# A hybrid recurrence and pooling block on eight cores: the pool group map, its channel scale and the pool part of the branch matrix multiplied into one matrix on the chip

## The reference, cut to what matters

```
proj = rmsnorm(h) @ w_in                      # q | f | i | out-gate | pool | gate_a | gate_b
ya = (rmsnorm_per_head(recurrence(q, f, i)) * sigmoid(og)) @ w_br_hgrn
# pool branch: 4 groups of 128 channels, windows 2, 4, 8, 16
pooled[g] = trailing_mean(xp[g], w_g) - xp[g]
y[g] = pooled[g] @ w_grp[g]                   # 128 x 128 for each group
yb = (y * scale) @ w_br_pool                  # 512 x 1024
h = h + (sigmoid(gate_a) * ya + sigmoid(gate_b) * yb) @ w_out
h = h + (silu(u @ w_gate) * (u @ w_up)) @ w_down      # u = rmsnorm(h), 2816 wide
out = rmsnorm(h)
```

## Time and profile before

| what | value |
|---|---|
| median of 3 runs | 2169.29 us (2168.22 to 2170.08) |
| the profiled execution's own time | 2170.29 us |
| its span, from the first to the last instruction, slowest core (core 5) | 2168.7 us |
| spans of the eight cores | 2158.5 to 2168.7 us |
| PE (matmul) busy | 2088.9 us, 96% of the span |
| DVE, ACT, POOL busy | 1001.8, 1007.0, 574.0 us |
| moved by DMA | 405.24 MB |

### The profile page before, as it was taken

How to read it: one execution, slowest core, us unless ns; L and a number is a source line. 1 busy time by engine, 2 the same in 40 slices (tenths; PEclk the granted TensorE clock), 3 DMA queues, 4 the chain that set the end, 5 groups by cost and what they waited for, 6 DMA issues and landing times.

```text
span 2168.7 us, 38075 instructions; the slowest of 8 cores (2158.5 to 2168.7 us)
## 1 busy us (share of the span) xinstructions
PE 2088.9 (96%) x11476; PEld 1106.8 (51%) x11476; DVE 1001.8 (46%) x1756; ACT 1007.0 (46%) x1492; POOL 574.0 (26%) x671
## 2 busy tenths in 40 slices
PE   6777998999999999999999999999999999999997
PEld 3432554555555555555555555555555555554447
DVE  4644453447534742474246523662357235732223
ACT  4832763258415742464247623662358324731111
POOL 3121120001105251423243143314332414223300
PEclk9988999999999999999999999999999999999999
DMA  9999999887565666557555755575557555565577
GB/s 202 211 198 249 217 223 238 228 213 221 147 183 154 186 190 177 158 156 225 170 151 170 223 162 159 168 222 162 166 164 199 180 173 158 165 175 174 169 197 191
DMA packets 232789, 405.24 MB, mean 187 GB/s; under 512 B 24208, under 2 KB 66704, under 8 KB 232592
## 3 DMA queue, kind: packets, MB, share of 16 engines
q1 hardware_dynamic: 210080, 364.62, 57.6%
q0 software_dynamic: 20880, 36.32, 11.7%
q10 hardware_dynamic: 1632, 1.88, 0.4%
HBM read 385.94 MB, written 53.08 MB: 202 GB/s over the span
## 4 chain that ended last, share of the span: by engine, by line
PE 84%; DMA 12%; SPq 1%; issue 1%; DVE 1%; ACT 1%; POOL 0%; DVEq 0%; POOLq 0%; ACTq 0%
PE psa L496 75%; DMA wsc<-wr 6%; DMA wr<-wpk 5%; PE psa L661 5%; DMA wr<-wsc 1%; PE psa L782 1%; SPq L364 1%; PE psa L796 1%; PE psa L815 1%; PE psa L816 1%; PE psa L831 0%; DMA fa<-xT 0%; PE psa L620 0%; PE psa L601 0%; DVE ba L630 0%
## 5 line engine op out<-in xcount | busy, mean ns | idle before, releaser
L496 PE MATMUL psa<-ba,wr 128*128 128x456 bf16 (+2 forms) x8960 | 1776.7, 354 | 19.8 <-DVE ba L546 6.6
L496 PEld LDWEIGHTS psa<-ba,wr 128*128 128x128 bf16 x8960 | 868.1, 98 | 830.2 <-issue 40.6
L906 DVE TENSOR_TENSOR ba<-psa,fa 128x456 bf16<-128x456 f32 (+1 forms) x198 | 124.5, 631 | 250.8 <-PE psa L496 213.0
L905 ACT ACTIVATE fa<-psa 128x456 f32<-128x456 f32 (+1 forms) x198 | 107.1, 551 | 217.1 <-PE psa L496 185.1
L589 POOL TENSOR_TENSOR fa<-fa 128x456 f32<-128x456 f32 (+1 forms) x160 | 158.0, 996 | 161.8 <-DMA fa<-xT 76.9
L773 POOL TENSOR_TENSOR ba<-fa 128x456 bf16<-128x456 f32 (+1 forms) x48 | 61.1, 1272 | 480.7 <-ACT fa L756 257.9
L363 POOL DMA_DIRECT2D wr<-wpk x145 | 76.8, 535 | 373.8 <-DMA wsc<-wr 180.6
L661 PE MATMUL psa<-wr,ba 128*114 128x512 bf16 (+1 forms) x576 | 136.6, 384 | 3.0 <-DMA wr<-wpk 3.0
L765 DVE TENSOR_TENSOR_SCAN fa<-ba,fa 128x456 f32<-128x456 bf16 (+1 forms) x72 | 83.4, 1159 | 120.1 <-ACT fa L763 120.0
L866 POOL TENSOR_TENSOR fa<-fa 128x456 bf16<-128x456 f32 (+1 forms) x48 | 55.3, 1152 | 289.2 <-DVE fa L863 289.2
L863 DVE SCALAR_TENSOR_TENSOR fa<-fa,psa 128x456 f32<-128x456 f32 (+1 forms) x72 | 45.3, 629 | 165.9 <-PE psa L496 165.9
(11 more groups left out here) (84 smaller groups left out, 1767.2 us busy)
## 6 DMA issues: line engine op xcount, KB each, us to landing
wr<-wsc SPq DMA_DIRECT2D x1040, 256.0 KB, 3.0
wr<-wpk POOLq DMA_DIRECT2D x128, 256.0 KB, 14.3
wsc<-wr SPq DMA_DIRECT2D x128, 256.0 KB, 18.3
wr<-wsc SPq DMA_DIRECT2D x72, 192.0 KB, 2.8
fa<-xT SPq DMA_DIRECT2D x6, 1824.0 KB, 13.9
outT<-fa SPq DMA_DIRECT2D x6, 1824.0 KB, 11.0
wr<-wsc SPq DMA_DIRECT2D x72, 128.0 KB, 2.3
fa<-xT SPq DMA_DIRECT2D x2, 1840.0 KB, 13.2
```

The costliest lines, as they stand in the source:

```text
L496: last = e.matmul(ps[bank][:, 0:c1 - c0], lhsT=sl[0].ap(i * 128, (i + 1) * 128), rhs=s_.ap(c0, c1), start=(start and i == 0), stop=(stop a ...
L905: yield act(lambda e: e.activation(out=sg.ap(0, nt), in_=ps[bg][:, 0:nt], func=AF.Silu), [PS(bg)], [sg.rg(0, nt)], tset="S", banks=[bg])
L906: yield dve(lambda e: e.tensor_tensor(out=ACT[fc].ap(0, nt), in0=ps[bu][:, 0:nt], in1=sg.ap(0, nt), op=ALU.mult), [PS(bu), sg.rg(0, nt)], ...
```

## The change: what it does

- The group matrices are handed over transposed (on the host, a change of layout), so that WGRP can be the stationary operand's source for a product with the branch matrix.
- Tile 0 gets a new stream, `s_fold`. After head 4 it scales the four transposed group matrices on ACT, one activation of 128 x 128 each, by PSCW along the partitions and puts them into U2, whose buffers are not used yet. Then, for each j, it multiplies the four blocks of WBPj by them (four matmuls of 128 x 128 into one bank), casts the bank's 512 columns on DVE back into WBPj's own slot, and puts the write-back of that slot into `pend`, so that `wsc` holds the product.
- The loads' own write-backs of WGRP and of WBP0 to WBP7 are left out; those of the eight products take the place of the latter.
- `s_merge` in tile 0 waits with the matmuls of WBPj for the flag of product j, and uses the slot as it is then. In tiles 1 to 8 it loads the products from `wsc`.
- `s_pool1` ends with POOLED[g], in all tiles: the four matmuls with WGRP, the four activations, and in tiles 1 to 8 the load of WGRP, are gone. `s_merge` reads POOLED (the same buffers as YP).

```diff
@@ issue_load @@
             if t == 0:
                 P.emit("pool", lambda e: e.dma_start(out=sbuf, in_=wpk[u, :, 0:n]), aft=early(), w=[sb.rg(0, n)], sem=f"v{slot}", inc=16, dma=True, dur=0.54, xfer=XL)
-                pend.append((slot, lambda: P.emit("sp", lambda e: e.dma_start(out=back, in_=sbuf), r=[sb.rg(0, n)], w=[(dk, 0, 1)], sem=f"b{slot}", inc=16,
-                                                  dma=True, dur=0.4, xfer=XB), nissue[0]))
+                if WU[u][1] not in ("grp", "brp"):
+                    pend.append((slot, lambda: P.emit("sp", lambda e: e.dma_start(out=back, in_=sbuf), r=[sb.rg(0, n)], w=[(dk, 0, 1)], sem=f"b{slot}", inc=16,
+                                                      dma=True, dur=0.4, xfer=XB), nissue[0]))
@@ s_pool1 @@
-                           [xp.rg(nt, nt + 16)], [HALO.rg(g * 16, (g + 1) * 16)], dur=0.2, flags=[("pooled", t, g)])
-            for g in range(4):
-                b = yield Bank()
-                yield Op("pe", lambda e, sl, b=b, g=g: e.matmul(ps[b][:, 0:nt], lhsT=sl[0].ap(g * 128, (g + 1) * 128), rhs=POOLED[g].ap(0, nt), start=True, stop=True),
-                         [POOLED[g].rg(0, nt)], [PS(b)], nt / 2400.0, units=[(t, "WGRP")], done=[(t, "WGRP")] if g == 3 else ())
-                yield act(lambda e, b=b, g=g: e.activation(out=YP[g].ap(0, nt), in_=ps[b][:, 0:nt], func=AF.Identity, scale=PSCW.ap(g, g + 1)),
-                          [PS(b), PSCW.rg()], [YP[g].rg(0, nt)], dur=0.66, banks=[b], flags=[("pool", t, g)])
+                           [xp.rg(nt, nt + 16)], [HALO.rg(g * 16, (g + 1) * 16)], dur=0.2, flags=[("pooled", t, g), ("pool", t, g)])
+        def s_fold():
+            yield Gate(("hs", 0, 4))
+            for g in range(4):
+                yield Op("act", lambda e, sl, g=g: e.activation(out=U2[g].ap(0, 128), in_=sl[0].ap(g * 128, (g + 1) * 128), func=AF.Identity, scale=PSCW.ap(g, g + 1)),
+                         [PSCW.rg()], [U2[g].rg(0, 128)], 0.3, units=[(0, "WGRP")], done=[(0, "WGRP")] if g == 3 else ())
+            for j in range(8):
+                yield Gate(("mix", 0, j - 3) if j >= 3 else ("hs", 0, 5))
+                key = (0, f"WBP{j}")
+                u = UIDX[f"WBP{j}"]
+                b = yield Bank()
+
+                def fold(e, sl, b=b):
+                    last = None
+                    for g in range(4):
+                        last = e.matmul(ps[b][:, g * 128:(g + 1) * 128], lhsT=U2[g].ap(0, 128), rhs=sl[0].ap(g * 128, (g + 1) * 128), start=True, stop=True)
+                    return last
+                yield Op("pe", fold, [U2[g].rg(0, 128) for g in range(4)], [PS(b)], 0.4, units=[key])
+                sb = SLOT[loaded[key]]
+                slot = loaded[key]
+                yield dve(lambda e, b=b, sb=sb: e.tensor_copy(out=sb.ap(0, 512), in_=ps[b][:, 0:512]), [PS(b)], [sb.rg(0, 512)], dur=0.7, banks=[b],
+                          flags=[("fold", j)])
+                pend.append((slot, lambda sb=sb, u=u, slot=slot: P.emit("sp", lambda e: e.dma_start(out=wsc[u, :, 0:512], in_=sb.ap(0, 512)), r=[sb.rg(0, 512)],
+                                                                        w=[(("dr", u), 0, 1)], sem=f"b{slot}", inc=16, dma=True, dur=0.4, xfer=XB), nissue[0]))
@@ s_merge @@
                 yield mm(b1, [(t, f"WGB{j}")], U, nt)
+                if t == 0:
+                    yield Gate(("fold", j))
                 b2 = yield Bank()
                 yield mm(b2, [(t, f"WBP{j}")], YP, nt)
@@ master @@
+                if t == 0:
+                    yield Spawn(1, s_fold())
                 yield Spawn(1, s_merge(t))
```

More of the change, by code:

```diff
@@ L1025 @@
             "out": np.asarray(w_out, np.float32)[0], "fg": np.asarray(w_ffn_gate, np.float32)[0], "fu": np.asarray(w_ffn_up, np.float32)[0],
-            "fd": np.asarray(w_ffn_down, np.float32)[0], "grp": np.asarray(w_pool_grp, np.float32)[0].reshape(512, 128)}
+            "fd": np.asarray(w_ffn_down, np.float32)[0], "grp": np.ascontiguousarray(np.asarray(w_pool_grp, np.float32)[0].transpose(0, 2, 1)).reshape(512, 128)}
     wpk = np.zeros((NU, 128, UW), np.float32)
```

## The result

The changed kernel takes **2190.8 us** (median of 5 runs), the kernel before 2169.3 us in the same comparison: ratio 1.0098, 95% interval 1.0086 to 1.0111. It is slower, by 21 us or 1%, where 2163.2 us and a gain were predicted. A second comparison gives 1.0108 (1.0091 to 1.0125).

A forecast was written before the change was run, and what follows sets the result against it. DMA was taken to bound the kernel before about 352 us, PE after. Removed matmuls -6.2, two DMAs -0.9 and SP's stops +1.0 sum to -6.1 us: 2163.2 us, own range 2160 to 2167, 8 in 10 range 2158 to 2172.

The forecast's parts named there:

- The gain of the removed matmuls: Tiles 1 to 8: 32 WGRP matmuls go from PE, each worth its distance of 0.1935 or 0.196 us; -6.2 us.
- the fourth rival: A freed matmul is worth less than its distance: weight loads set PE's pace, 3.1 us gained, 2166.3 us; chance 0.02.
- its own test: Prediction wrong if the distance from PE's last DMA wait in tile 1 to the end shrinks by something other than 6.2 us.
- The -0.9 us for the two DMAs: DMA-bound start: tile 1's WGRP load and tile 0's WGRP write-back go, 0.45 us each; -0.9 us.
- Tile 0: Added small matmuls, casts and activations in tile 0, hidden by the DMA-bound part behind; taken as 0, uncovered 2 to 7 us.
- SP's stops: Tile 0: SP waits for DVE's casts before write-backs, 14 us near 104 and 24 us near 120; +1.0 us.
- a sign of being wrong: Prediction wrong if the DMA share dips between 110 and 160 us.
- That rival: SP starves DMA: its two stops empty its queue, DMA-bound stretch ends 11.8 us later, 2174.0 us; chance 0.12.
- The waits at the border: PE's waits for tile 1's loads before 343 and 352 us; rival: they go, 6.0 us more gained, 2157.2 us; chance 0.10.
- the second rival: New order makes PE wait: 0.5 us in each of tiles 2 to 8, 3.5 us given back, 2166.7 us; chance 0.16.

The follow-up runs named there:

- e1: Kernel before without WGRP's matmuls, activations and load in tiles 1 to 8; planner still counts their time (old order), no products in tile 0: 2164.1 us, ratio 0.9979.
- e3: Whole change, tile 0's products included, but the planner counts the dropped steps' time in tiles 1 to 8, keeping the old order: 2164.8 us, 0.9982 of before.
- e12: Changed kernel, replanned freely: U2 products after the last feed-forward product, U products after GpSimd's squares from tile 4, other slacks and margins: 2163.3 us, ratio 0.9975.
- e4: As e3, but the products' write-backs stand up to 16 loads later in SP's list, other engines' orders unchanged: 2165.0 us, ratio 0.9983 to the kernel before.
- e5: The changed kernel run again unaltered, against the kernel before: 2192.1 us, ratio 1.0108.
- e2: Kernel before with the same steps as in e1 left out of tiles 1 to 8, but the planner orders freely: 2174.1 us, ratio 1.0025.
- e7: Changed kernel, same order on every engine, GpSimd's norm squares and sums over 16 columns instead of 456: 2178.2 us, ratio 1.0044 to the kernel before.
- e10: As e3, in the old order, but GpSimd's norm squares and sums cover 16 columns instead of 456: 2164.1 us, ratio 0.9979 to the kernel before.

## Why the prediction was wrong

**The gain of the removed matmuls** (-6.2 us) was right: from before to e1, in the same order, the rest shrinks by 6.1 us (1788.9 to 1782.8), so a matmul is worth its distance, and the fourth rival (3.1 us) falls. The prediction named this distance as its own test; in the change it grows by 17.8 us. In whole times e3, which does the whole change, takes 3.9 us less than before and e12 5.4 us less, where 6.1 were predicted; the intervals of both (1.7 to 6.3 and 3.5 to 7.6 us) take that in. The -0.9 us for the two DMAs is too small for any run here to show by itself.

**Tile 0** (taken as 0) was right: e3 and e1 differ by 0.7 us. **SP's stops** (+1.0) cost nothing that e3 and e4 can tell apart. The stops are there. On the slowest core SP issues nothing from 104.7 to 127.3 us, predicted as 14 us from 104, and nothing from 134.5 to 154.8 us, predicted as 24 us from 119 (on core 0 they last from 100.6 to 121.2 and from 128.1 to 147.7 us). SP's issues on both sides of the second, slowest core:

```profile
131.91 2.63 SPq L365 DMA_DIRECT2D wsc<-wr  x4
154.82 0.32 SPq L739 DMA_DIRECT2D wsc<-wr  x1
```

The DMA share dips, which the prediction named as a sign of being wrong; e4, without most of the dip, is no faster. The sign was badly chosen: a dip would matter only where PE's last wait for DMA comes later by it. That rival (2174.0, with the DMA-bound stretch 11.8 us longer) has the wrong mechanism.

**The waits at the border** vary with the core: in e5 they are 2.8 us on core 0 and 1.2 us on core 5, in the kernel before 1.0 us on core 0 and 6.0 us on core 5. They decide nothing here.

**The step that failed** is the new order. The sum, -6.2 - 0.9 + 1.0, has no term for it, so it stands at nothing there; it appears only as the second rival, "the new order makes PE wait". That rival named the right mechanism and had the size wrong by a factor of five or more: "one wait of 0.5 us in each of tiles 2 to 8", 3.5 us, with a chance of 0.16, because there are "0.3 us of waits in seven tiles now, and only work is removed". Measured between the same work in the old order and in the new are 18.3 us of gaps and 4.3 us of half-rate matmuls, 22.6 us, on core 0, 23.7 us of the rest on the median core, and 27 us in the time of the slowest core. Both reasons were mistaken. The 0.3 us were not a cover but the outcome of one particular order, and the change kept that order nowhere after the first tile; the bound of a wait in a new order is not the smallest wait seen elsewhere but what can stand ahead of a needed instruction in its queue, here eight products of 0.62 us, 4.9 us, and 10.1 us where they collide. And "only work is removed" is true of the instructions and false of a greedy planner. e1 to e2 shows it with nothing added: 10 us lost by planning freely around less work. The rival's place was right too ("ACT and DVE ... in bursts"): a burst of eight norm products is what holds PE up. The trace of before could have priced the collision: L630 takes 0.62 us each in one batch and 0.785 us on the mean of its 80 of 456 columns, because in every other batch of eight two products have GpSimd beside them and the eight take 6.6 us.

## What to carry to other kernels

Where a planner or scheduler decides the order, a small edit is two changes, the work and the plan; price them apart, and measure them apart by keeping the removed operations as time only. A trace without waits says that this order fits and not that there is room (the kernel before had collisions in six tiles, all hidden): before trusting it, ask for each queue what batch can stand ahead of the instruction that the bottleneck waits for. A planner's durations have to hold beside the other engines' work too; here 0.69 us in the table was 0.62 us alone and 1.27 us beside GpSimd, and a rule that keeps the two apart won back 29 us together with one for U2 and four other constants (which of these did how much was not tried; the rule for U2 alone gave 2187.8 us).

## What the runs showed of the hardware

- VectorE's product of two SBUF operands (128 x 456, fp32) takes 0.62 us alone and 1.27 us, on the mean of eight, beside GpSimd's two-input operations, which go from 0.95 and 1.15 us to 1.15 and 1.36 us (the change, core 0, 1286 us; e7 shows it alone in the same place). Shortening GpSimd's squares and sums gains 14 us in one order (e7) and nothing in another (e10).
- A wait of TensorE of 4.1 us is followed by matmuls at a granted clock of 0.66 on the mean over 5 us (core 0; 0.52 to 0.72 on cores 1 to 5); over all waits after 450 us core 0 of the change loses 4.3 us more in slow matmuls than e3, beside 18.3 us more of gaps.
- SP issued nothing for some 20 us twice in the DMA-bound part of e3, with the DMA share down to 0.33 to 0.83 over 10 us, and e4, without most of the dip (0.72 to 1.03), takes the same time.
